# A hybrid Mamba-2 and sparse-attention layer: the high and low parts of each weight tile interleaved word by word, and the two operands of a matmul placed 256 bytes apart

## What is computed

```python
h = _rmsnorm(x, g_pre) * (1.0 + scale[:, None, :]) + shift[:, None, :]
z_ssm, xbc, dt_raw, q, kv, nsa_gate, z_att, merge_gate = jnp.split(h @ w_in, IN_SPLITS, axis=-1)
y_ssm = _mamba2_branch(z_ssm, xbc, dt_raw, conv_w, conv_b, dt_bias, a_log, d_skip, g_ssm_norm) @ w_ssm_out
y_nsa = _nsa_branch(q, kv, nsa_gate, z_att, ...) @ w_nsa_out
mg = jax.nn.sigmoid(merge_gate.reshape(bsz, s, N_BRANCH, dm))
merged = mg[:, :, 0] * y_ssm + mg[:, :, 1] * y_nsa
out = merged @ w_out
return x + gate[:, None, :] * _rmsnorm(out, g_post)
```

## Time and profile before

| | us |
|---|---|
| median of 3 runs (lowest, highest) | 493.61 (493.58, 495.37) |
| profiled execution | 492.43 |
| its span, first instruction to last | 490.6 |
| TensorE busy in the span | 448.6 (91%) |
| VectorE busy | 350.1 (71%) |
| ScalarE busy | 267.8 (55%) |
| GpSimd busy | 232.7 (47%) |
| mean granted TensorE clock, share of full speed | 0.982 |

### The profile page before, as it was taken

The page is one execution under the profiler, slowest core; times in us unless marked ns, Lnnn a source line. Parts: engine busy times, 40 slices in busy tenths (PEclk is TensorE's granted clock), DMA queues, the critical chain, the costliest instruction groups (busy, mean ns, idle before and its releaser), DMA issues.

```text
span 490.6 us, 9766 instructions
## 1 busy us (share of the span) xinstructions
PE 448.6 (91%) x3592; PEld 409.9 (84%) x3592; DVE 350.1 (71%) x611; ACT 267.8 (55%) x518; POOL 232.7 (47%) x238
## 2 busy tenths in 40 slices
PE   0759989999999989997879899999999999999995
PEld 0439989999999879996779889888999898999874
DVE  0167989598999989888867986846565766549643
ACT  1354776555585585735485674555746564445441
POOL 0043453458476847985353563244444543335340
PEclk9987998999999999999999998999999999999999
DMA  8976444633435235326856782325243333356402
GB/s 307 425 298 228 160 138 154 190 122 130 174 124 173 91 112 190 114 104 229 328 184 246 265 294 87 126 89 173 92 134 123 132 126 130 130 180 222 156 2 86
DMA packets 21959, 82.99 MB, mean 169 GB/s; under 512 B 2444, under 2 KB 2834, under 8 KB 20626
## 3 DMA queue, kind: packets, MB, share of 16 engines
q1 hardware_dynamic: 21912, 82.37, 47.6%
HBM read 81.31 MB, written 1.05 MB: 168 GB/s over the span
## 4 chain that ended last, share of the span: by engine, by line
PE 67%; issue 8%; POOL 7%; DMA 7%; DVE 5%; ACT 4%; SPq 1%; DVEq 0%; POOLq 0%; ACTq 0%
PE gemm L617 17%; PE gemm L618 16%; PE gemm L619 16%; DMA w_raw<-in_wpack 7%; PE y_or_o L814 2%; ACT w_hi L843 2%; POOL cmp_blocks L459 2%; POOL w_lo L1412 1%; PE y_or_o L696 1%; PE score L778 1%; PE score L780 1%; SPq L472 1%; DVE w_lo L1092 1%; PE small L564 1%; PE small L566 1%
## 5 line engine op out<-in xcount | busy, mean ns | idle before, releaser
L1412 POOL TENSOR_TENSOR w_lo<-w_raw,w_hi 128x256 fp32r<-128x256 f32 (+1 forms) x117 | 133.6, 1147 | 173.5 <-ACT w_hi L843 167.8
L617 PE MATMUL gemm<-h_hi,w_hi 128*128 128x256 f32 x680 | 198.9, 293 | 4.5 <-DVE w_lo L1092 2.3
L618 PE MATMUL gemm<-h_lo,w_hi 128*128 128x256 f32 x680 | 192.9, 284 | 0.0
L619 PE MATMUL gemm<-h_hi,w_lo 128*128 128x256 f32 x680 | 192.5, 283 | 0.0
L1092 DVE TENSOR_TENSOR w_lo<-w_raw,w_hi 128x768 fp32r<-128x768 f32 (+1 forms) x117 | 128.2, 1098 | 58.8 <-ACT w_hi L843 58.6
L843 ACT CAST w_hi<-w_raw 128x1024 fp32r<-128x1024 f32 x117 | 122.1, 1045 | 45.7 <-PE gemm L619 27.9
L617 PEld LDWEIGHTS gemm<-h_hi,w_hi 128*128 128x128 f32 x680 | 130.8, 192 | 8.3 <-issue 7.3
L618 PEld LDWEIGHTS gemm<-h_lo,w_hi 128*128 128x128 f32 x680 | 130.9, 193 | 0.6
L619 PEld LDWEIGHTS gemm<-h_hi,w_lo 128*128 128x128 f32 x680 | 130.5, 192 | 0.0
L1141 DVE SCALAR_TENSOR_TENSOR conv_acc<-gemm,conv_half,conv_acc 128x255 f32<-128x255 f32 (+2 forms) x72 | 34.5, 480 | 8.2 <-ACT conv_acc L877 6.2
L617 PE MATMUL gemm<-ynorm_hi,w_hi 128*128 128x256 f32 x128 | 36.5, 285 | 0.0
(11 more groups left out here) (233 smaller groups left out, 780.0 us busy)
## 6 DMA issues: line engine op xcount, KB each, us to landing
w_raw<-in_wpack SPq DMA_DIRECT2D x133, 512.0 KB, 3.4
w_ada_shift_scale<-in_w_ada SPq DMA_DIRECT2D x8, 1024.0 KB, 15.1
x_T<-in_xT SPq DMA_DIRECT2D x1, 1024.0 KB, 10.6
x_residual<-in_x_tok SPq DMA_DIRECT2D x1, 1024.0 KB, 7.9
out_tok_dram<-out_tok SPq DMA_DIRECT2D x4, 256.0 KB, 2.1
consts<-in_consts SPq DMA_DIRECT2D x1, 272.0 KB, 22.6
cmp_bias_and_valid<-in_cmp_bias SPq DMA_DIRECT2D x1, 272.0 KB, 6.1
w_compress<-in_w_compress SPq DMA_DIRECT2D x1, 192.0 KB, 5.5
```

Of the source, the lines that this page charges most:

```text
L617: nc.tensor.matmul(bank[:, 0:SEQ], w_hi, hi[:, k0 + k, :], start=first, stop=False)
L618: nc.tensor.matmul(bank[:, 0:SEQ], w_hi, lo[:, k0 + k, :], start=False, stop=False)
L619: last = nc.tensor.matmul(bank[:, 0:SEQ], w_lo, hi[:, k0 + k, :], start=False, stop=end)
L1412: nc.gpsimd.tensor_tensor(WL[:, n % LO_SLOTS, c:1024], RAW[:, u % RAW_SLOTS, c:1024], WH[:, n % HI_SLOTS, c:1024], ALU.subtract).then_inc( ...
```

## The change

It moves no instruction on any engine and changes no wait. It does three things.

- `WH` and `WL` become one tensor `W` of four slots with 2048 words each. In all units but those of the output projection, word 2i of a slot holds the high part of weight i and word 2i+1 the low part, so that ScalarE, VectorE and GpSimd read and write them with a step of 8 bytes, and a stationary tile of 128 columns spans 1024 bytes. In the output projection's units the high part is the slot's first half and the low part its second, contiguous as before.
- The addresses modulo 512: `W` starts at 384, the split activations and the raw slots start at 128.
- Small tensors (`mod`, `eps_columns`, `ada_scale`, `gate_times_g`, `softmax_small`) stand elsewhere, the extra pads of 64, 64 and 384 bytes are gone, and the whole upper part of the memory lies 320 bytes lower.

```diff
@@ -211,6 +211,8 @@
 OUT_K = 2
 OUT_N = 512
 AHEAD = LO_SLOTS - 1
+LINES = 512
+MOVING, LOADED = 128, 384
 
 
 def lo_share(n):
@@ -232,25 +234,29 @@
             cursor[0] += size
         return nc.alloc_sbuf_tensor_at(name, shape, dt, offset=off)
 
+    def home(remainder):
+
+        cursor[0] += (remainder - cursor[0]) % LINES
+        return cursor[0]
+
+    h_at = home(MOVING)
+    HH = place("h_hi", [P, KT, SEQ], f32r)
+    HL = place("h_lo", [P, KT, SEQ], f32r)
+    RAW = place("w_raw", [P, RAW_SLOTS, 1024], f32)
     MOD = place("mod", [P, 16], f32)
     EPSC = place("eps_columns", [P, 3], f32)
     AB = place("ada_scale", [P, 16], f32)
     GG = place("gate_times_g", [P, 2, 8], f32)
-    cursor[0] += 64
-    h_at = cursor[0]
-    HH = place("h_hi", [P, KT, SEQ], f32r)
-    HL = place("h_lo", [P, KT, SEQ], f32r)
-    RAW = place("w_raw", [P, RAW_SLOTS, 1024], f32)
-    SM = place("softmax_small", [P, 2, 4, 4], f32)
-    cursor[0] += 64
-    WH = place("w_hi", [P, HI_SLOTS, 1024], f32r)
-    WL = place("w_lo", [P, LO_SLOTS, 1024], f32r)
+    home(LOADED)
+    W = place("w_hi_lo", [P, HI_SLOTS, 2048], f32r)
+    assert HI_SLOTS == LO_SLOTS
     PR = place("params", [P, PAR["end"][1]], f32)
     CS = place("consts", [P, CST["end"][1]], f32)
     IDB = place("ident_bf16", [P, P], bf16)
     MSL = place("mask_sl_bf16", [P, P], bf16)
     MQK = place("mask_qk_bf16", [P, P], bf16)
     CW = place("conv_half", [P, 120], f32)
+    SM = place("softmax_small", [P, 2, 4, 4], f32)
     GATE = place("att_gate", [P, 2, ATT_HEADS, 3], f32)
     ys_at = cursor[0]
     F0 = place("dt_gate_T", [P, SEQ], f32)
@@ -261,9 +267,9 @@
     TP = place("acs_rows", [P, 2, P], f32)
     ST = place("acs_cols", [P, 3, P], f32r)
     AEX = place("exp_a_log", [P, SSM_HEADS], f32)
-    cursor[0] = ys_at + 8192 + 384
+    cursor[0] = ys_at + 8192
     YS = place("y_ssm_out", [P, 8, SEQ], f32, at=ys_at)
-    z_at = cursor[0]
+    z_at = home(MOVING)
     Z = place("z_gate_then_y", [P, 16, SEQ], f32)
     YNH = place("ynorm_hi", [P, 16, SEQ], f32r, at=z_at)
     YNL = place("ynorm_lo", [P, 16, SEQ], f32r)
@@ -335,6 +341,12 @@
     SSO = place("out_sq_sums", [P, 2, 2], f32, at=q_at + 24 * kb)
     RO = place("rstd_out", [P, 2, 3], f32, at=q_at + 24 * kb + 64)
     XR = place("x_residual", [P, 2, D_MODEL], f32, at=over_at + 28 * kb)
+
+    def weights(n, half, lo=0, hi=1024):
+
+        if UNITS[SPLIT_UNITS[n]][0] == "out":
+            return W[:, n % HI_SLOTS, 1024 * half + lo:1024 * half + hi]
+        return W[:, n % HI_SLOTS, half + 2 * lo:half + 2 * hi - 1:2]
 
     def par(name, lo=0, hi=None):
         a, b = PAR[name]
@@ -558,8 +570,8 @@
                     else:
                         for m in range(2):
                             wait_small_out(pe, ("pt", ATT_HEADS - 1, m))
-                w_hi = WH[:, n % HI_SLOTS, OUT_N * kk:OUT_N * kk + OUT_N]
-                w_lo = WL[:, n % LO_SLOTS, OUT_N * kk:OUT_N * kk + OUT_N]
+                w_hi = weights(n, 0, OUT_N * kk, OUT_N * kk + OUT_N)
+                w_lo = weights(n, 1, OUT_N * kk, OUT_N * kk + OUT_N)
                 hi, lo = MH[:, k, P * t:P * t + P], ML[:, k, P * t:P * t + P]
                 nc.tensor.matmul(bank[:, :], hi, w_hi, start=(k == 0), stop=False)
                 nc.tensor.matmul(bank[:, :], hi, w_lo, start=False, stop=False)
@@ -611,8 +623,8 @@
                         pe.wait_ge(h_ready, k + 1)
                     if kind == "nsa" and j == 0:
                         pe.wait_ge(o_split, k + 1)
-                    w_hi = WH[:, n % HI_SLOTS, P * k:P * k + P]
-                    w_lo = WL[:, n % LO_SLOTS, P * k:P * k + P]
+                    w_hi = weights(n, 0, P * k, P * k + P)
+                    w_lo = weights(n, 1, P * k, P * k + P)
                     first, end = (k == 0 and part == 0), (k == KT - 1 and part == parts - 1)
                     nc.tensor.matmul(bank[:, 0:SEQ], w_hi, hi[:, k0 + k, :], start=first, stop=False)
                     nc.tensor.matmul(bank[:, 0:SEQ], w_hi, lo[:, k0 + k, :], start=False, stop=False)
@@ -840,7 +852,7 @@
                 act.wait_ge(w_in[u % RAW_SLOTS], 16 * (u // RAW_SLOTS + 1))
                 if n >= HI_SLOTS:
                     act.wait_ge(unit_mm, n - HI_SLOTS + 1)
-                nc.scalar.copy(WH[:, n % HI_SLOTS, :], RAW[:, u % RAW_SLOTS, :]).then_inc(hi_ready, 1)
+                nc.scalar.copy(weights(n, 0), RAW[:, u % RAW_SLOTS, :]).then_inc(hi_ready, 1)
 
             def tanh_half(tile, src, rows=P):
 
@@ -1089,8 +1101,7 @@
                 if n >= LO_SLOTS:
                     dve.wait_ge(unit_mm, n - LO_SLOTS + 1)
                 c = P * lo_share(n)
-                nc.vector.tensor_tensor(WL[:, n % LO_SLOTS, 0:c], RAW[:, u % RAW_SLOTS, 0:c], WH[:, n % HI_SLOTS, 0:c],
-                                        ALU.subtract).then_inc(lo_ready, 1)
+                nc.vector.tensor_tensor(weights(n, 1, 0, c), RAW[:, u % RAW_SLOTS, 0:c], weights(n, 0, 0, c), ALU.subtract).then_inc(lo_ready, 1)
 
             def gate(tile, out_ap, src, rows=P):
 
@@ -1409,8 +1420,7 @@
                 pool.wait_ge(hi_ready, n + 1)
                 if n >= LO_SLOTS:
                     pool.wait_ge(unit_mm, n - LO_SLOTS + 1)
-                nc.gpsimd.tensor_tensor(WL[:, n % LO_SLOTS, c:1024], RAW[:, u % RAW_SLOTS, c:1024], WH[:, n % HI_SLOTS, c:1024],
-                                        ALU.subtract).then_inc(lo_rest_ready, 1)
+                nc.gpsimd.tensor_tensor(weights(n, 1, c), RAW[:, u % RAW_SLOTS, c:1024], weights(n, 0, c), ALU.subtract).then_inc(lo_rest_ready, 1)
 
             for n in range(AHEAD):
                 split_lo_rest(n)
```

## The result

The changed kernel takes **499.76 us** (median of 4 runs, 498.82 to 503.39) beside 493.65 for the kernel before (4 runs): ratio 1.0139, 95% interval 1.0103 to 1.0175. It is slower, and lies outside the range. The profiled execution took 498.8 us, with a span of 497.0 against 490.6 before.

The account below looks back on a forecast made before the run. The prediction took TensorE's matmul pace as the bound, DVE close behind in the middle. Savings of 13.5 us on gemm matmuls and 1.3 on the output projection made 14.8 off 493.6, so 479 us, range 468 to 496.

Parts of the forecast that it names:

- What bounds the kernel: Whole kernel: the pace of TensorE's matmuls sets the end, TensorE busy 91%, with DVE close behind in the middle.
- The pace has two levels: Lines 617 to 619: 118.0 or 113.6 ns a matmul; about 4 ns depend on how load and stream meet.
- Rival A: Gemm matmuls: nothing changes, both levels come from issue after a wait; 118 ns stay, 493 to 494 us; 13%.
- The new pace lies between 107 and 113.6 ns: 2,616 gemm matmuls: 111 ns taken, 7.0 ns less each, 18.3 us, of which 13.5 kept; 66%.
- Now they run at equal speed, and a distance once good stays good.: Gemm matmuls: stationary and moving tiles both span 1,024 bytes, so load and stream need no longer pass each other.
- The floor: TensorE: least pace where little is streamed, 107 ns from 8 transposes and 113 ns from 16 narrow products.
- the least that this instruction has shown: Gemm matmuls: 113.6 ns, seen in a fast unit before the change, taken as upper end of the new pace.
- Rival B: Every gemm matmul: load and stream collide twice as long, 11 ns more each, 29 us, 522 us; 14%.
- The output projection: Its 96 matmuls of 512 columns go from 233 to 219 ns, saving 1.3 us, all on the path.
- Writing word by word: Splits on ACT, DVE and POOL: accesses with a step of 8 bytes were taken to cost nothing.
- Rival C: Splits get dearer, 0.7 ns a word on DVE; about 12 to 15 us lost, 499 us; 7%.
- The shift of the rest: Other PE work: all other operands shift by one amount, mostly 448 to 128; nothing put there.

Follow-up runs that it names:

- e6: Kernel before with contiguous weights, other operands at the change's addresses, load starting 52 bytes (modulo 256) from the stream in place of 192: 488.79 us, ratio 0.9884.
- bench: Separate kernel computing no layer: streams of 24 matmuls at varied load-to-stream distances, contiguous and stepped; contiguous 120.0 ns at distance 0, 117.8 at 192.
- e1: The change without interleaving: high and low weights in two contiguous tensors, load and stream still 256 bytes apart; 497.26 us, ratio 1.0091.
- bench4: Separate kernel computing no layer: all 64 word distances, one entry each; stepped loads 117.8 to 122.2 ns, contiguous 113.3 to 120.3.
- e4: The change with ACT's copy cut from 1,024 to 928 words after the first four units; 500.01 us, ratio 1.0144.
- e3: The change's addresses for everything else, but contiguous weights and 192 bytes between load and stream; ratio 0.9995 to the kernel before.
- 224: Kernel with contiguous weights and the change's other addresses, load 224 bytes from the stream in place of 192; 494.15 us, ratio 1.0033.
- e7: Kernel before with contiguous weights, other operands at the change's addresses, load 76 bytes from the stream in place of 192; 491.32 us, ratio 0.9957.

## Why the prediction was wrong, point by point

**What bounds the kernel: right.** The pace of lines 617 to 619 sets the end. From #1728 to #2592, where the clock is level, the milestones move by pace x count to 0.2 us: 1.9 us later in the change, 2.2 us earlier in e6. Of the span's 6.4 us, 2.4 are waits that are not traced to the pace.

**"The pace has two levels ... they depend on how the weight load and the stream meet in time": right, but it does not carry "the resource which this edit touches".** The bench shows 113.3 and 117.8 with nothing else running. But both appear at one and the same distance (64, 180 and the kernel's own 192), by what ran ahead of the unit. So the fast unit of the earlier trace rows was no sign that addresses were at fault. That the addresses matter as well is shown by 192 against 0, 117.8 against 120.0. Rival A falls with that: e1 moves the kernel's pace from 117.69 to 119.8 by the distance alone. Its mechanism was issue after a wait, and the units of the bench have none; but that the two levels do not come from the addresses was right. The Trainium skill (TensorE: Matmul & The Clock Gate, the step on LDWEIGHTS) has two independent read ports, by which the distance between load and stream should not matter; the measurements decide against that as a rule of time.

**"The new pace lies between 107 and 113.6 ns": the step that failed.** It measured 119.98. Three things in it were wrong:

- *"Now they run at equal speed, and a distance once good stays good."* I named this as a reading, and then let no part of the range stand on its opposite. It assumed that the distance was good. Contiguous loads at the change's distance run at 120.0, among the slowest of all 64 (e1 and bench4). Nor does equal speed keep anything good: the fast level was not met at any stepped distance.
- *The floor.* The 107 and 113 of the earlier trace rows belong to contiguous loads. A stepped load beside only 128 streamed columns took 117.8, which is above my whole range of paces. Nothing in the trace of before showed a stepped load, and that was the unknown cost to be bounded from both sides. I had the rule of the Trainium skill ready beside the splits (SBUF — State Buffer, the note on cachelines: two accesses to each 16-byte line are enough) and did not hold it against the load, where the runs show otherwise: 8 bytes cost 6.1 ns of 111.7, and 16 bytes double it to 233.
- *113.6 as "the least that this instruction has shown", and so the upper end.* It was shown (113.3 by the unrounded starts) in three units at the old distance. A level that held in three units of 109 says that it exists, not that a new layout will find it.

**Rival B: right in its place and sign, not in its size.** The price of 29 us came from doubling an 11 ns excess over the floor; the excess grew by 2.3 ns, 6.0 us. Its own condition ("over 118 by 1 ns, 2.6 us") was met. Had I priced it from what was near, a few ns between levels as in the earlier trace rows, 4.4 ns x 2,616 = 11.5 us would have been the bound, and a range up to 505 us would have held the result.

**The output projection: sign right, size off.** Forecast 219 ns, measured 227: 0.6 us in place of 1.3. It comes from the distance, since e1 has 227 as well; with 512 streamed columns distance 0 is a good one in the bench (227.7 against 232.7 at 64).

**Writing word by word: right for DVE (+13 ns) and POOL (+23), wrong for ACT.** I put nothing; the copy takes 90 ns more (62 alone). "Its cover is 45% idle time" is not settled: taking the 90 ns away in e4 changed nothing measurable, but a gain of some 2 us can hide in the clock there. Rival C had 1.5 us for DVE's low part and fell with the 1,057 ns.

**The shift of the rest: right**, by e3, within its interval of 0.3%.

**What was not foreseen: waits, and the scatter of the clock.** 2.4 us of the change's loss in the profiled execution are waits of PE, for which the sum had no term of loss. The clock dips in every profile, at different places, for 1.7 to 3.4 us at a time. It took 1.8 us less from the change than from the kernel before, so it is no cause of the loss, but it is large enough to hide an effect of this size in single executions.

## What to carry to other kernels

When a stream of matmuls with a load each sets the end, its pace from start to start is a quantity to measure by placement: a bench that sends the same pair at every word distance costs one run, found a distance that made this kernel 0.7 to 1.2% faster, and would have ruled out both halves of this change. Send each pair behind more than one entry: the pace also hangs on what ran ahead. A pace seen in a few units of a trace is no promise for a new layout, and a floor read from one form of load is no floor for another. Take the winner of a bench back into the full kernel before believing it: 224 did not carry over, and 76 had the best pace but no better time than 52. And compare the mean granted clock of the runs before a difference of a few us is given a cause.

## What the runs showed of the hardware that was not expected

- The pace of a 256-column float32r stream with 128-column loads depends on the distance of their starts (repeating every 256 bytes in steps of 64), and at distance 192 on no absolute place (117.7 to 117.9 at seven places). It jumps between 113.3 and 123.3 ns from one 4-byte word to the next. Why 52 and 76 are good is open.
- At some distances (64, 180, and the kernel's 192) two paces, 113.3 and 117.8, are both possible, and what runs ahead of a unit decides between them. With 32 columns loaded at distance 0 it was 120.0 in one bench and 113.3 in another.
- With streams of 128 to 240 columns the distance did not matter: 111.5 to 112.1 ns at distance 0 as at 192.
- A step of 8 bytes costs the weight load 6 ns in 112, a step of 16 bytes doubles it (221.5 with 32 columns streamed, 233 with 256). The same 8-byte step costs ACT's write 62 ns in 1,044, DVE's nothing (959) and POOL's nothing in 722, or 13 where it reads with the step too.
- After PE's wait near 180 us the granted clock differed between kernels with waits of 3.4 to 3.9 us: 1.00 throughout in e1, 0.76 and 0.56 in the change, 0.50 and 0.83 in e7. The kernel before dipped at 298 us while PE had run without a gap for 15 us. A dip of 3.4 us costs as much as 1.3 ns on every gemm matmul.
